# Rounding and subtracting weight pieces in pairs in a float32 hybrid attention and delta-rule block

## The reference

```python
def reference(x, w_in, ..., w_out, ln_mix_pre, ln_mix_post, w_up, ..., w_down, ln_ffn_pre, ln_ffn_post):
    h = x
    for l in range(DEPTH):
        m = token_mixer(rmsnorm(h, ln_mix_pre[l]), w_in[l], ..., w_out[l])
        h = h + rmsnorm(m, ln_mix_post[l])
        f = conv_ffn(rmsnorm(h, ln_ffn_pre[l]), w_up[l], ffn_conv_w[l], ffn_conv_b[l], w_down[l])
        h = h + rmsnorm(f, ln_ffn_post[l])
    return h

def token_mixer(xn, w_in, ...):
    proj = jnp.einsum('btd,dc->btc', xn, w_in)                  # 2048 -> 7168 + 16 columns
    ...
    o_sb = stick_breaking_attention(q, k, v)                    # 8 heads of 128
    o_sb = rmsnorm(o_sb, sb_out_gain)
    dn_qkv = jax.nn.silu(causal_dwconv(dn_qkv, dn_conv_w))      # width 4
    o_dn = gated_delta_rule(l2norm(q), l2norm(k), v, g, beta)   # 8 heads of 128
    o_dn = rmsnorm(o_dn, dn_out_gain) * jax.nn.silu(dn_z)
    return jnp.einsum('btc,cd->btd', concatenate([o_sb, o_dn]), w_out)

def conv_ffn(xn, w_up, ffn_conv_w, ffn_conv_b, w_down):
    h = causal_dwconv(jnp.einsum('btd,df->btf', xn, w_up), ffn_conv_w) + ffn_conv_b
    gate, val = jnp.split(h, 2, axis=-1)
    return jnp.einsum('btf,fd->btd', jax.nn.gelu(gate, approximate=True) * val, w_down)
```

## Time and profile before

| | |
|---|---|
| median of 3 runs | 1225.43 us (1225.20 to 1225.55) |
| the profiled execution | 1225.67 us, its span 1223.9 us |
| granted clock of TensorE, mean | 0.998 of full |
| TensorE busy | 1204.1 us, 98% |
| VectorE busy | 888.9 us, 73% |
| ScalarE busy | 729.7 us, 60% |
| GpSimd busy | 196.8 us, 16% |
| read from HBM | 224.91 MB, 186 GB/s over the span |

### The profile page before, as it was taken

How to read it: one execution, slowest core, us unless ns; L and a number is a source line. 1 busy time by engine, 2 the same in 40 slices (tenths; PEclk the granted TensorE clock), 3 DMA queues, 4 the chain that set the end, 5 groups by cost and what they waited for, 6 DMA issues and landing times.

```text
span 1223.9 us, 19897 instructions
## 1 busy us (share of the span) xinstructions
PE 1204.1 (98%) x6499; PEld 1031.7 (84%) x6499; DVE 888.9 (73%) x1703; ACT 729.7 (60%) x1438; POOL 196.8 (16%) x242
## 2 busy tenths in 40 slices
PE   8999999999999999999999999999999999999997
PEld 5888898888888888888888888888888888888886
DVE  5889986875457556887887888888888875555554
ACT  6877466646786546756656656665665554454542
POOL 1131111010221000122222231232222210000000
PEclk9999999999999999999999999999999999999999
DMA  9646434643434553555555555545554565555541
GB/s 362 264 182 225 165 115 130 229 170 141 143 144 183 189 201 138 187 192 187 190 180 197 193 184 198 179 174 203 180 197 173 204 241 178 200 198 185 202 172 69
DMA packets 34885, 227.79 MB, mean 186 GB/s; under 512 B 5504, under 2 KB 5904, under 8 KB 8208
## 3 DMA queue, kind: packets, MB, share of 16 engines
q1 hardware_dynamic: 33536, 224.48, 51.0%
q10 hardware_dynamic: 1296, 2.61, 0.6%
HBM read 224.91 MB, written 2.17 MB: 186 GB/s over the span
## 4 chain that ended last, share of the span: by engine, by line
PE 86%; DVE 8%; ACT 3%; DMA 2%; issue 1%; SPq 0%; POOL 0%; DVEq 0%; ACTq 0%; POOLq 0%
PE bank L1424 32%; PE bank L1428 16%; PE bank L1450 10%; PE bank L1452 10%; PE bank L1451 10%; DVE w_lo L920 3%; DMA arena<-in_x_tok 2%; DVE arena L941 2%; ACT w_hi L478 1%; PE bank L1553 1%; PE bank L1703 1%; PE bank L1702 1%; PE bank L1701 1%; DVE arena L925 0%; PE bank L1537 0%
## 5 line engine op out<-in xcount | busy, mean ns | idle before, releaser
L920 DVE TENSOR_TENSOR w_lo<-raw,w_hi 128x512 fp32r<-128x512 f32 x816 | 567.8, 718 | 238.2 <-ACT w_hi L478 235.8
L478 ACT ACTIVATE w_hi<-raw 128x512 fp32r<-128x512 f32 x816 | 502.3, 630 | 357.8 <-PE bank L1424 184.3
L1424 PE MATMUL bank<-xhl,w_hi 128*128 128x512 f32 x2028 | 650.1, 398 | 6.0 <-DVE arena L925 4.1
L1428 PEld LDWEIGHTS bank<-xhl,w_lo 128*128 128x128 f32 x2028 | 381.3, 188 | 87.8
L1428 PE MATMUL bank<-xhl,w_lo 128*128 128x256 f32 x2028 | 398.8, 278 | 0.0
L1424 PEld LDWEIGHTS bank<-xhl,w_hi 128*128 128x128 f32 x2028 | 313.0, 189 | 8.2 <-DVE w_lo L920 5.9
L1452 PE MATMUL bank<-w_hi,ffn_act 128*128 128x512 f32 x336 | 130.7, 389 | 0.0
L1451 PE MATMUL bank<-w_lo,ffn_act 128*128 128x512 f32 x336 | 130.7, 389 | 0.0
L1450 PE MATMUL bank<-w_hi,ffn_act 128*128 128x512 f32 x336 | 130.7, 389 | 0.0
L445 POOL TENSOR_TENSOR arena<-arena,token_scale 128x256 f32<-128x256 f32 x88 | 78.6, 908 | 299.4 <-DVE arena L925 191.4
L1340 DVE SCALAR_TENSOR_TENSOR arena<-arena,fcw 128x256 f32<-128x256 f32 x176 | 85.3, 484 | 23.9 <-DVE arena L1340 1.5
(11 more groups left out here) (255 smaller groups left out, 962.6 us busy)
## 6 DMA issues: line engine op xcount, KB each, us to landing
raw<-in_wts SPq DMA_DIRECT2D x203, 1024.0 KB, 4.8
xfeat<-in_x SPq DMA_DIRECT2D x4, 512.0 KB, 10.0
arena<-in_x_tok SPq DMA_DIRECT2D x1, 2048.0 KB, 20.2
xfeat<-in_x_tok SPq DMA_DIRECT2D x1, 2048.0 KB, 9.2
out_y<-xfeat SPq DMA_DIRECT2D x8, 256.0 KB, 2.0
arena<-gate_rows SPq DMA_DIRECT2D x1, 1024.0 KB, 4.4
arena<-base_rows SPq DMA_DIRECT2D x4, 256.0 KB
arena<-in_post_gains ACTq DMA_DIRECT2D x1, 1024.0 KB, 4.8
```

The costliest lines, as they stand in the source:

```text
L478: nc.scalar.activation(w_hi[:, i % RING, :], raw[:, slot, quarter * PIECE:(quarter + 1) * PIECE], ACT.Copy).then_inc(hi_ready, 1)
L920: V.tensor_tensor(w_lo[:, i % RING, :], raw[:, slot, quarter * PIECE:(quarter + 1) * PIECE], w_hi[:, i % RING, :].bitcast(f32), ALU.subtra ...
L1424: return M(ps[j][:, :], w_hi[:, r % RING, kk * P:(kk + 1) * P], xhl[:, k, :, :].rearrange("p a t -> p (a t)"), start=(k == 0), stop=(k == ...
L1428: return M(ps[j][:, 0:T], w_lo[:, r % RING, kk * P:(kk + 1) * P], xhl[:, CHUNK_K * q + kk, 0, :], start=False, stop=False, skip_group_chec ...
```

## The change

`split_width(g, i)` says how many pieces the split at piece i of group g handles: one for the first six of the first group, otherwise two for an even i and none for an odd i. The rounding on ScalarE and the subtraction on VectorE cover 1024 columns of `raw`, `w_hi` and `w_lo` at once; since the rings have 8 pieces and a chunk 4, the two pieces of a pair lie side by side in all three. Semaphores are advanced by two. The rounding of pieces i and i+1 waits for `piece_used` of i+2, so until TensorE has finished piece i-7. The places of all other work are as before; only the slots of odd i are empty. TensorE's, GpSimd's and SP's lists are unchanged.

```diff
+def split_width(g, i):
+    if isinstance(g, int) and g == 0 and i < AHEAD:
+        return 1
+    return 0 if i % 2 else 2
...
         def _(act_e):
             def split(g, i):
+                n = split_width(g, i)
+                if n == 0:
+                    return
                 slot, quarter = (i // 4) % RAW, i % 4
...
-                act_e.wait_ge(piece_used, g * 16 + (i + 1))
-                nc.scalar.activation(w_hi[:, i % RING, :], raw[:, slot, quarter * PIECE:(quarter + 1) * PIECE], ACT.Copy
-                                     ).then_inc(hi_ready, 1)
+                act_e.wait_ge(piece_used, g * 16 + (i + n))
+                nc.scalar.activation(w_hi[:, i % RING:i % RING + n, :].rearrange("p a c -> p (a c)"),
+                                     raw[:, slot, quarter * PIECE:(quarter + n) * PIECE], ACT.Copy).then_inc(hi_ready, n)
...
             def split(g, i):
+                n = split_width(g, i)
+                if n == 0:
+                    return
                 slot, quarter = (i // 4) % RAW, i % 4
-                dve.wait_ge(hi_ready, g * 16 + (i + 1))
-                V.tensor_tensor(w_lo[:, i % RING, :], raw[:, slot, quarter * PIECE:(quarter + 1) * PIECE],
-                                w_hi[:, i % RING, :].bitcast(f32), ALU.subtract).then_inc(lo_ready, 1)
+                dve.wait_ge(hi_ready, g * 16 + (i + n))
+                V.tensor_tensor(w_lo[:, i % RING:i % RING + n, :].rearrange("p a c -> p (a c)"),
+                                raw[:, slot, quarter * PIECE:(quarter + n) * PIECE],
+                                w_hi[:, i % RING:i % RING + n, :].rearrange("p a c -> p (a c)").bitcast(f32), ALU.subtract
+                                ).then_inc(lo_ready, n)
```

## The result

The changed kernel takes **1237.22 us** (median of 4 executions, 1237.12 to 1237.38) against 1225.4 us before (1225.2 to 1225.55): ratio 1.0097, 95% interval 1.0079 to 1.0114. The prediction was 1226.7 us with a range up to 1229.6, so the time lies outside it. Its profiled execution has a span of 1235.6 us against 1223.9.

What follows compares the result with a forecast made beforehand. TensorE, busy 98% of the span, was taken to bound the kernel. Terms +0.2 (start's remainder), -1.0, +1.2 and +0.95 gave +1.35, say 1.3, on 1225.43: 1226.7 us, range 1223.7 to 1229.6.

Steps and rivals of the forecast that it cites:

- What bounds the kernel, and where it is decided: Whole kernel: TensorE, busy 98%, bounds it; the change is decided before 400 us, with 0 from later projections and the end.
- The prices: All pairs: 1.06 us, step 0.94, on ScalarE; 1.22, step 1.13, on VectorE; 0.08 and 0.07 cheaper than two singles.
- The start, +1.0 to +1.1: Up to 36.36 us: pair (8, 9) delays TensorE 0.96; the diagonal behind slot 12's pair absorbs nothing; 1.0 to 1.1 late.
- 88.61 and 142.91 "nearly absorbed", 0 to 0.25 left: TensorE's waits at 88.61 and 142.91 us: the start's delay shrinks to 0.4, then to 0 to 0.25 us.
- 199 to 202, -1.0: Bank additions near 199 to 202 us: of 1.66+0.79 us waiting, 1.0 is won, since bank 1's stands behind a pair.
- The batches, +1.2 and +0.95: At 343 and 391 us: pairs at even slots wait one piece longer, delaying head scaling and later handoffs; +1.2 and +0.95.
- the four it named: Batch handoffs counted: first transposes 1.0, next scores 0.2, second transposes 0.8, and z_hi and z_lo before 391.09's successor, ending 392.0.
- The slower rival: Handoffs after even slots cost more than counted, 2.3 us per batch; +4.7 less cover, 1229.5 us; chance 24%.
- three things that I had called signs of being wrong: No new wait in 340 to 395 us, a wait in the up or down projection, or a ScalarE pair at 1.2 or more.
- the new waits that I had named: Near 344 and 383 us for L1197's successor, 0.5 to 1.2 us each, and a longer one near 392.
- The range: Whole kernel's time: 1223.7 to 1229.6 us, from the lower side of "nothing" to the slower rival, to hold 8 in 10.

Runs made afterwards that it cites:

- e11: e7 with pieces 6 to 11 single, so that the start is as before: 1236.0 us.
- e5: Changed kernel with pairs on ScalarE alone; VectorE subtracts 512 columns at a time as before the change: 1232.12 us.
- e7: Changed kernel plus two matmuls on constants, adding no result, in TensorE's wait at place 82: 1235.73 us.
- e10: e7 with two pieces of 816 single, 198 and 199: 1234.4 us.
- e4: Changed kernel with both pieces of each pair taken at the odd slot, keeping that slot's earlier wait for TensorE: 1230.32 us.

## Why the prediction was wrong, step by step

- **What bounds the kernel, and where it is decided**: right. The loss is complete at 403 us. The up and down projections and the end gave 0, as said.
- **The prices**: right. I took 1.06 and 0.94 us (end and step) on ScalarE, 1.22 and 1.13 on VectorE. In the changed kernel a rounding takes 1.06 and three in a row 3.01, a step of 0.98 at most (two at the closest 1.99, 0.93); a subtraction takes 1.25 in the mean and two in a row 2.35, a step of 1.1.
- **The start, +1.0 to +1.1**: right in size, +0.96 at 37.32, of which 0.76 at piece 8, and right in its reason: the diagonal stands behind the pair of slot 12. Its rounding starts when it did before (34.41 against 34.48), and the two longer operations make the diagonal 0.96 later. e11, which keeps this pair and takes the earlier ones away, has it as late.
- **88.61 and 142.91 "nearly absorbed", 0 to 0.25 left**: wrong, as the list of handoffs was short here too, and this is the first of the two large misses, +3.67 at place 82. I followed VectorE's row of work between the two stops and priced the saving of seven pairs. What I left out were the handoffs between them that had no wait before, and those ahead of the first stop: place 28 (0.55 us for L1044; the lag is 1.64 us behind it, and the wait at 89.53 takes 0.7 back), place 60, where ScalarE's activation L539 stands behind the pair of an even slot (0.81, and in e5 the same 0.81 without any pair on VectorE; the lag grows by 0.97), and at place 82 bank additions behind pairs of 1.5 and 1.6 us instead of single ones (the lag grows by 1.62). e5's lag of 2.07 there against 3.67 puts some 1.6 us on VectorE's pairs and the rest on ScalarE's side.
- **A clock drop** behind the longer wait: not in the prediction at all, +1.5 (e7).
- **199 to 202, -1.0**: wrong in size, -0.25 (5.23 to 4.98). The direction of its parts was right: in e5, where no bank addition stands behind a pair on VectorE, the wait at 199 is gone and the lag falls by 1.75 (2.07 to 0.32). In the changed kernel the two waits are 0.93 and 1.32 instead of 1.66 and 0.79: the pair ahead of the second addition takes nearly everything back. I had expected 0.2 for the first. The key norms did come 1 us earlier against TensorE, but behind them VectorE still takes a pair, which waits for its rounding until 200.50, and only then the triangles and the addition.
- **The batches, +1.2 and +0.95**: wrong, +3.3 (4.98 to 8.31) and +3.4 (8.31 to 11.70). The places that I named are there: L1211 makes TensorE wait 0.66 at 351.57 and 0.32 at 392.59, and `mix_hl` 1.02 at 402.79. Missing are the masks of POOL (0.78 and 1.00) and the token evacuation (1.10, worth 1.33 by e10). By the growth of the lag, the handoffs that I named cost 2.95 us (1.16 at the first transposes, 0.45 at the next scores, 0.85 at the second transposes, 0.49 at `mix_hl`) where I had 2.15, and those that I left out 3.67 (masks 1.06 and 1.27, evacuation 1.34). **This is the step that failed: the sum took the handoffs behind a pair to be the four it named, and put all others, at which the trace shows no wait, at nothing.** Its terms were a little small; its list of terms was short by more than half.
- **The slower rival** had the right mechanism, "the handoffs after even slots cost more than I count", and too small a price: 1.1-1.0+4.6 with the cover taken off. It multiplied the places that I already had instead of asking for others. None of the three things that I had called signs of being wrong came either: the new waits that I had named are there (351, 392 and 403 us), and no sign on my list asked for waits elsewhere.
- **The range**: its upper end was that rival's, and held no case for a handoff that I hadn't looked at.

One term stays partly open. At place 82 and at 91 us some subtractions of 1024 columns took 1.54 to 1.80 us. VectorE in the changed kernel, and POOL in the same stretch:

```profile
140.42 1.54 DVE L932 TENSOR_TENSOR w_lo<-raw,w_hi 128x1024 fp32r<-128x1024 f32 x1 [0.35 <-ACT w_hi L487]
141.88 0.74 DVE L939 TENSOR_TENSOR arena<-bank,half 128x256 f32<-128x256 f32 x2
142.55 1.64 DVE L932 TENSOR_TENSOR w_lo<-raw,w_hi 128x1024 fp32r<-128x1024 f32 x1
144.12 0.41 DVE L939 TENSOR_TENSOR arena<-bank,half 128x256 f32<-128x256 f32 x1
...
140.15 0.72 POOL L386 TENSOR_TENSOR arena<-arena,token_scale 128x256 f32<-128x256 f32 x1 [19.42 <-DVE arena L939]
142.38 3.10 POOL L386 TENSOR_TENSOR arena<-arena,token_scale 128x256 f32<-128x256 f32 x3 [1.50 <-DVE arena L939]
```

All 30 subtractions of over 1.4 us in the changed kernel overlap a POOL operation on two tensors; none of the 314 that overlap no POOL work is that slow, but 61 beside such a product aren't slow either. In the kernel before the singles there took 0.88 to 0.90 us instead of 0.68 while POOL was at the same work. The Trainium skill (SBUF — State Buffer, SBUF: two separate sides) says that a VectorE operation with two inputs in SBUF contends with a GpSimd operation that reads SBUF, and that the loser waits for the whole of the other. The trace fits the contention: 0.2 us more for a single and 0.3 to 0.6 for a pair here; it does not show a wait for the whole of a product, which takes 0.7 to 1.2 us. No run here took POOL's work away, so that this makes the pairs' cost at place 82 is argued, not shown.

## What to carry to other kernels

When an operation is made longer or waits for a later event, list **every** handoff behind it on that engine, also those at which nobody waits in the profile: a wait appears only once a handoff is missed. What each has to spare is read from the end of the producer's row to the start of the consumer's, less that distance where the consumer does wait. This kernel, with an engine 98% busy, gained at most 1.0 us from shorter work on the others, and the wait for one more piece alone, without any grouped work, cost over half as much as the grouping did. Group only where nobody stands behind the group, and put the group at the slot where its last member stood (e4: 5.0 us lost instead of 11.8).
